# Start of the kernel and differential attention: sums moved from TensorE to VectorE, a new order of projections and heads

## The chip, the cores and the metric

The kernel runs on one core of one Trainium2 chip. The metric is the device time of one execution in microseconds (us). TensorE (PE) multiplies matrices, VectorE (DVE) and ScalarE (ACT) work element by element, GpSimd (POOL) and SyncE (SP) issue transfers here.

## The reference

Two transformer blocks over 256 tokens of width 1024 are computed, all in float32. What the change touches:

- The first block's modulation: `mod = silu(c) @ w_mod + b_mod`, six vectors of 1024. The first norm is `h = rms_norm(x, norm_mix) * (1 + scale_m) + shift_m`, and then `z = h @ w_in`.
- The second block's first layer, differential attention over 256 context tokens and 256 own tokens, 8 heads of two maps each:

```python
q, k, v = split(h @ w_qkv)            # for own and context tokens
q_l, k_l = axial_rope(q_l), axial_rope(k_l)
s = einsum('bqhnd,bkhnd->bnhqk', q, k) * scale
p = softmax(s)
a = p[:, 0] - lam * p[:, 1]
o = rms_norm_2(einsum('bhqk,bkhe->bqhe', a, v), subln_g) * (1 - lam_init)
x = x + g1 * (o @ w_o)
```

Before it stand a mixer with two attentions and a recurrence, its branch projections and a gated feed-forward layer; behind it a dense feed-forward layer, a Fourier mixer and eight experts, of which each token uses two.

## The kernel before, in words

**Weights.** All weights come through SP as slabs of 1 MB into raw buffers (`raw`, four slots, at the start three more that lie where `O` and `GT1` are later). A weight slab "G" is split in two parts, since a product is made of three passes: ACT copies it to `whi` (L1234, `act_hi`), DVE subtracts and writes `wlo` (L1812, `dve_lo`), and then PE has it. There are three such pairs, so the split of slab g+3 waits until PE is through slab g. A slab of the modulation weights "M" isn't split: DVE multiplies its rows by the entries of `csil` and adds them up in `macc` (L1836 for the first, L1839 for the others, `dve_mslabs`), and PE sums over the partitions with four short matmuls (L696, `pe_mods`), whose result DVE adds to the bias (L1857, `dve_mods`). The raw slot is free for SP when DVE has read it. The order of all slabs is the list `st_order`, the slots of the first ten are the list `early`.

**The start.** The first four modulation vectors' groups (2, 3, then 0, 1; two M slabs each) don't go this way: `pe_direct` (L710) multiplies each raw slab on PE, 16 weight loads with a moving operand of one column. Groups 2 and 3 give the scale (`dve_coeff`), 0 and 1 the shift. `pe_start` goes: transpose of `csil`'s rows, group 2, a transpose of vectors, group 3, the transposes of x (L747) with the sums of squares (L723, L726), group 0. The modulated x is written by `modulation`: `scaled` (L1878, DVE), high part `HH` (L1276, ACT), low part `HL` (`low`, L1885, DVE). `pe_mixer` multiplies the first two slabs together, chunk k by chunk k (`gemm2`, L625 to L627), and does group 1 between k = 3 and k = 4.

**Differential attention.** `pe_attention`, `act_attention` and `dve_attention` walk through 25 units. Each quarter c of the columns has five: k over context tokens, k over own tokens, q, v over context, v over own, each 48 matmuls of 256 columns (20 units, 12 slabs). After each unit the engines do `side(unit)`: rotations (`pe_rope` L963, `dve_rope` L2197 to L2205), the steps of heads, and modulation sums. A head h has steps 0 to 4, at units 5·(h // 2) + 4 + h % 2 onward: scores of query block 0 (PE L939, DVE maximum L2215), scores of block 1 and transposes of block 0 (PE L929), transposes of block 1, values (L947), norm (L952). Two heads run one unit apart, and the last ones in units 20 to 24, which have no projection. Between, DVE's side is in two parts: the maxima before `dve_lo` and `dve_mslabs`, the softmax's division and difference (L2221 to L2227) behind them, while ACT does the exponentials (L1559). At the end all heads are split to `HH2` and `HL2` (L1379, L2021), and the output projection "wo" runs over its four slabs one after the other. PE's PSUM banks are taken in rings: four for projections (`A_G`), three for the heads (`A_T`), one for the sums of squares (`A_L`); a bank is taken only after its last reader is done.

Everything is written out by hand: each engine works its list in order, and waits are semaphores.

Of the kernel before, what the change touches and what calls it, by code (L numbers as in the profile page):

```python
# [15 lines left out]
S = 256  # L16
# [183 lines left out]
def build(nc, a, out):  # L200
# [5 lines left out]
    with ctx:  # L206
# [121 lines left out]
        raw_read = Count(sem("raw_read_by_pe"))  # L328
# [41 lines left out]
        for c in range(4):  # L370
            for c0 in (4 + c, c, 8 + c):
                order += gslabs(wqkv, 8, 256 * c0, ("qkv", c0))
# [20 lines left out]
        st_order = first[:4] + order[0:2] + first[4:] + order[2:3]  # L393
# [4 lines left out]
        early = (6, 7, 8, 0, 1, 2, 3, 6, 7, 8)  # L398
        for i, entry in enumerate(st_order):
            st.add(entry, early[i] if i < 10 else (i - 10) % NR)  # L400
# [25 lines left out]
        for i, entry in enumerate(order):  # L426
            s_ = i % (NR + NX)
            st.add(entry, (s_ + first_moe - 10) % NR if s_ < NR else s_)
# [10 lines left out]
        direct = {i for i, (kind, t, *_) in enumerate(st.plan) if kind == "M" and t[0] == 0 and t[1] < 4}  # L439
# [52 lines left out]
        HEAD0 = 6  # L492
        SPANS = ((0, 128), (128, 256))


        def sp_weights(q, i0, i1):
            for i in range(i0, i1):
                _, _, src, nk, w = q.plan[i]
                s_ = q.slot[i]
                if q is st and q.prev[i] in direct:  # L500
                    sp.wait_ge(*(yield from raw_read.of(q.prev[i])))
                elif q.prev[i] is not None:
# [155 lines left out]
        def gemm2(ring, keys, tags, xh, xl, ready, between=None):  # L658
# [5 lines left out]
            for k in range(8):  # L664
                if between and k == 4:
                    between()
# [21 lines left out]
        def pe_mods(ring, slot):  # L688

            while due(pmod[0], slot):  # L690
# [8 lines left out]

        def pe_direct(ring, n):  # L700

            d, g, last, _ = mlist[n]
            u = take(ring, "mod", n)
            for i in (last - 1, last):
                pe.wait_ge(st.raw_in[st.slot[i]], 16 * st.use[i])
                v = raw[st.slot[i]][:, :].rearrange("p (k n) -> p k n", k=4)
                for j in range(4):
                    for k in range(4):
                        kk = 4 * (i + 1 - last) + k
                        t = pe.matmul(u.t[:, j:j + 1], v[:, k, j * 128:(j + 1) * 128], csil[:, kk:kk + 1], start=(j == 0 and kk == 0),  # L710
                                      stop=(kk == 7), skip_group_check=True)
                t.then_inc(raw_read.mark(i), 1)
            u.told = raw_read.now()
            pmod[0] = n + 1
# [16 lines left out]
        def pe_start():  # L731
# [4 lines left out]
            pe.wait_ge(*(yield from N.of("csil")))  # L736
            pe_direct(Z_T, 0)
# [3 lines left out]
            pe_direct(Z_T, 1)  # L741
# [11 lines left out]
            pe_direct(Z_T, 2)  # L753
# [81 lines left out]
        def pe_mixer():  # L835
            yield from gemm2(Z_G, (("z", 0), ("z", 1)), (("z", zjob[0][2]), ("z", zjob[1][2])), HH, HL,
                             lambda k: xlo_done.of("h0", k), lambda: pe_direct(Z_T, 3))
# [82 lines left out]
        A_G, A_T, A_L = (0, 1, 2, 3), (4, 5, 6), (7,)  # L920

        def pe_da(h, step):

            for qb in range(2):
                if step == qb + 1:
                    u = take(A_T, "a_p", h, qb)
                    pe.wait_ge(*(yield from dve_step.of("a_p", h, qb)))
                    for j in range(4):
                        t = pe.transpose(u.t[:, j * 128:(j + 1) * 128], PP[(2 * h + qb) % 3][:, 0, j * 128:(j + 1) * 128], ident)  # L929
                    t.then_inc(u.fill(), 1)  # L930
            for qb in range(2):
                if step == qb:
                    if step == 0:
                        pe.wait_ge(*(yield from dve_step.of("rope", "q", h // 2)))
                        pe.wait_ge(*(yield from dve_step.of("rope", "k", h // 2)))
                    for n in range(2):
                        u = take(A_T, "a_s", h, qb, n)
                        r0 = 64 * n
                        pe.matmul(u.t[:, :], Q2[r0:r0 + 64, h, qb * 128:qb * 128 + 128], K2[r0:r0 + 64, h, :],  # L939
                                  start=True, stop=True).then_inc(u.fill(), 1)  # L940
            if step == 3:
                u = take(A_T, "a_o", h)
                for n in range(2):
                    pe.wait_ge(*(yield from N.of("v2", h // 2, n)))
                    pe.wait_ge(*(yield from N.of("at", h, n)))
                for j in range(4):
                    t = pe.matmul(u.t[:, 0:S], V2[:, j, h * 128:(h + 1) * 128], AT[h % 2][:, j, :], start=(j == 0), stop=(j == 3))  # L947
                t.then_inc(u.fill(), 1)
            if step == 4:
                u = take(A_T, "a_n", h)  # L950
                pe.wait_ge(*(yield from sq_done.of("a", h)))
                pe.matmul(u.t[:, 0:S], one[:, :], sqb[h % 2][:, 0:S], start=True, stop=True).then_inc(u.fill(), 1)  # L952
                N.note(("sq_free", "a", h), u.told)
# [12 lines left out]
        def pe_attention():  # L966
            def side(unit):
                c, k = divmod(unit, 5)
                if k == 2 and c < 4:
                    yield from pe_rope("k", c)  # L970
                if k == 3 and c < 4:
                    yield from pe_rope("q", c)
                for h in range(8):
                    step = unit - (5 * (h // 2) + 4 + h % 2)
                    if 0 <= step < 5:
                        yield from pe_da(h, step)
                yield from pe_mods(A_T, st.slab_done.n - 1)

            for c in range(4):
                h, l, nk = yield from slab(st, ("qkv", 4 + c))  # L980
                us = [take(A_G, "k2", c, m) for m in range(2)]
                for n, (xh, xl, name) in enumerate(((HHc, HLc, "hc"), (HH2, HL2, "h2"))):
# [7 lines left out]
                    if n:  # L990
                        t.then_inc(st.slab_done.mark(st.pg - 1), 1)
                        us[0].told = us[1].told = st.slab_done.now()
                    yield from side(5 * c + n)
                yield from gemm(A_G, ("q2", c), ("qkv", c), 1, HH2, HL2, None, 7)
                yield from side(5 * c + 2)
                h, l, nk = yield from slab(st, ("qkv", 8 + c))
                for n, (xh, xl) in enumerate(((HHc, HLc), (HH2, HL2))):
                    u = take(A_G, "v2", c, n)
# [1675 lines left out]
```

## Time and profile before

| | |
|---|---|
| median of 3 runs | 2256.78 us (2253.92 to 2257.61) |
| the profiled execution | 2251.45 us, its span 2250.1 us |
| PE busy | 2140.3 us (95% of the span) |
| DVE busy | 1689.0 us (75%) |
| ACT busy | 1260.5 us (56%) |
| granted TensorE clock, mean | 0.963 of full |
| DMA | 580.73 MB, mean 258 GB/s |
| share of PE in the chain that ended last | 83% (DVE 9%, ACT 4%) |

Matmuls overlap in the pipeline, so a duration in the timeline is longer than the distance to the next start: of the 256-column matmuls each is shown as 0.28 us, and the next begins 0.12 us later at full clock. Distances between starts are the measure of what PE costs. A row's bracket tells how long the engine was idle before it, and what ended that.

### The profile page before, as it was taken

The page shows a single profiled execution, that of the slowest core. Times are in us where ns is not written, and L with a number is a line of the kernel's source. Part 1 is how long each engine was busy: PE and PEld are TensorE (multiplying, and loading weights), DVE is VectorE, ACT ScalarE, POOL GpSimd, SP SyncE. Part 2 cuts the span into 40 slices and gives each one's busy share as a digit, 9 for nine tenths or more (in the row PEclk, how much of TensorE's full clock was granted, in tenths as well). Part 3 has the DMA queues.
Part 4 walks back from the last instruction along what each step waited for, and adds up shares of the span by engine and source line. Part 5 has one row for each costly group of instructions (what it writes and reads, how often), then busy time and mean ns, then how long its engine had stood idle before and what let it go on. Part 6 is the DMA issues. An engine that isn't in the chain of part 4 may idle for free.

```text
span 2250.1 us, 31050 instructions
## 1 busy us (share of the span) xinstructions
PE 2140.3 (95%) x12897; PEld 1897.6 (84%) x12897; DVE 1689.0 (75%) x1809; ACT 1260.5 (56%) x1266; POOL 39.4 (2%) x77
## 2 busy tenths in 40 slices
PE   8999999989999978999998999999999999999997
PEld 8887899889997866999988788887888878888886
DVE  1477688699765664787644888888888978888886
ACT  2347753545343433434343677776777767777775
POOL 3001000000000000000000000000000000000000
PEclk9899999989999988999998999999999999999999
DMA  8574476467764332688843899999899989999994
GB/s 280 169 223 114 134 244 208 155 203 252 239 199 138 113 127 80 217 302 273 272 132 122 301 355 355 364 352 362 318 357 357 362 318 357 363 355 362 367 369 154
DMA packets 332802, 580.73 MB, mean 258 GB/s; under 512 B 10357, under 2 KB 150155, under 8 KB 332656
## 3 DMA queue, kind: packets, MB, share of 16 engines
q1 hardware_dynamic: 329152, 572.57, 73.0%
q0 software_dynamic: 3008, 5.78, 1.1%
q8 instruction: 105, 1.72, 0.3%
q10 hardware_dynamic: 496, 0.33, 0.1%
q14 instruction: 41, 0.34, 0.0%
HBM read 577.56 MB, written 1.07 MB: 257 GB/s over the span
## 4 chain that ended last, share of the span: by engine, by line
PE 83%; DVE 9%; ACT 4%; issue 3%; DMA 0%; SPq 0%; DVEq 0%; ACTq 0%
PE bk L631 14%; PE bk L633 14%; PE bk L632 14%; PE bk L625 9%; PE bk L627 9%; PE bk L626 9%; DVE macc L1839 2%; DVE wlo L1812 2%; PE bk L710 2%; ACT whi L1234 2%; PE bk L696 1%; PE bk L1126 1%; DVE uc L2154 1%; PE bk L681 1%; PE bk L683 1%
## 5 line engine op out<-in xcount | busy, mean ns | idle before, releaser
L1812 DVE TENSOR_TENSOR wlo<-raw,whi 128x2048 fp32r<-128x2048 f32 x475 | 1080.6, 2277 | 281.7 <-ACT whi L1234 281.0
L1234 ACT CAST whi<-raw 128x2048 fp32r<-128x2048 f32 x475 | 902.4, 1901 | 413.3 <-PE bk L633 271.6
L625 PE MATMUL bk<-HH,whi 128*128 128x256 f32 x1544 | 454.0, 294 | 11.3 <-DVE HL L1885 8.3
L626 PE MATMUL bk<-HL,whi 128*128 128x256 f32 x1544 | 443.8, 287 | 0.0
L627 PE MATMUL bk<-HH,wlo 128*128 128x256 f32 x1544 | 443.5, 287 | 0.0
L631 PE MATMUL bk<-whi,xh 128*128 128x512 f32 x896 | 356.9, 398 | 4.9 <-DVE wlo L1812 4.9
L633 PE MATMUL bk<-wlo,xh 128*128 128x512 f32 x896 | 351.4, 392 | 0.0
L632 PE MATMUL bk<-whi,xl 128*128 128x512 f32 x896 | 351.0, 392 | 0.0
L625 PEld LDWEIGHTS bk<-HH,whi 128*128 128x128 f32 x1544 | 304.0, 197 | 20.6 <-issue 17.9
L626 PEld LDWEIGHTS bk<-HL,whi 128*128 128x128 f32 x1544 | 304.1, 197 | 1.7 <-issue 1.0
L627 PEld LDWEIGHTS bk<-HH,wlo 128*128 128x128 f32 x1544 | 303.5, 197 | 0.0
L631 PEld LDWEIGHTS bk<-whi,xh 128*128 128x128 f32 x896 | 169.6, 189 | 40.1 <-DVE wlo L1812 6.6
L633 PEld LDWEIGHTS bk<-wlo,xh 128*128 128x128 f32 x896 | 169.4, 189 | 36.3
L632 PEld LDWEIGHTS bk<-whi,xl 128*128 128x128 f32 x896 | 169.7, 189 | 33.8
L1839 DVE SCALAR_TENSOR_TENSOR macc<-raw,csil,macc 128x512 f32<-128x512 f32 x252 | 188.9, 751 | 7.7
L631 PE MATMUL bk<-whi,tth 128*128 128x512 f32 x448 | 177.5, 396 | 1.7 <-DVE ttl L2437 1.7
L633 PE MATMUL bk<-wlo,tth 128*128 128x512 f32 x448 | 177.7, 397 | 0.0
L632 PE MATMUL bk<-whi,ttl 128*128 128x512 f32 x448 | 177.5, 396 | 0.0
L625 PE MATMUL bk<-FH,whi 128*128 128x256 f32 x400 | 114.3, 286 | 0.0
L626 PE MATMUL bk<-FL,whi 128*128 128x256 f32 x400 | 113.1, 283 | 0.0
L627 PE MATMUL bk<-FH,wlo 128*128 128x256 f32 x400 | 113.0, 283 | 0.0
L631 PEld LDWEIGHTS bk<-whi,tth 128*128 128x128 f32 x448 | 84.3, 188 | 22.1 <-DVE ttl L2437 1.9
(366 smaller groups left out, 2579.3 us busy)
## 6 DMA issues: line engine op xcount, KB each, us to landing
raw<-in_moe_w SPq DMA_DIRECT2D x336, 1024.0 KB, 5.7
raw<-in_ada_w SPq DMA_DIRECT2D x48, 1024.0 KB, 5.2
raw<-in_ff_w SPq DMA_DIRECT2D x40, 1024.0 KB, 5.4
raw<-in_w_in SPq DMA_DIRECT2D x29, 1024.0 KB, 5.4
raw<-in_w_mod SPq DMA_DIRECT2D x24, 1024.0 KB, 5.5
raw<-in_w_up SPq DMA_DIRECT2D x22, 1024.0 KB, 5.2
raw<-in_attn_w_qkv SPq DMA_DIRECT2D x12, 1024.0 KB, 5.3
raw<-in_w_branch SPq DMA_DIRECT2D x8, 1024.0 KB, 5.3
```

What stands on the lines that cost most here:

```text
L625: pe.matmul(o, sh, mh, start=start, stop=False, skip_group_check=True)
L626: pe.matmul(o, sh, ml, start=False, stop=False, skip_group_check=True)
L627: return pe.matmul(o, sl, mh, start=False, stop=stop, skip_group_check=True)
L631: pe.matmul(o, sh, mh, start=start, stop=False, skip_group_check=True)
L632: pe.matmul(o, sl, mh, start=False, stop=False, skip_group_check=True)
L633: return pe.matmul(o, sh, ml, start=False, stop=stop, skip_group_check=True)
L681: pe.matmul(o, xh[:, k, c], h[:, k, :], start=(k == 0), stop=False)
L683: t = pe.matmul(o, xh[:, k, c], l[:, k, :], start=False, stop=(k == 7))
L710: t = pe.matmul(u.t[:, j:j + 1], v[:, k, j * 128:(j + 1) * 128], csil[:, kk:kk + 1], start=(j == 0 and kk == 0), stop=(kk == 7), skip_grou ...
L1234: act.copy(whi[k][:, :n], raw[q.slot[i]][:, :n]).then_inc(q.hi_done.mark(g), 1)
L1812: dve.tensor_tensor(wlo[k][:, :n], raw[q.slot[i]][:, :n], whi[k][:, :n].bitcast(F), ALU.subtract).then_inc(q.taken.mark(i), 1)
L1839: t = dve.scalar_tensor_tensor(out=acc[:, :], in0=v[:, j, :], scalar=sc, in1=acc[:, :], op0=ALU.mult, op1=ALU.add)
```

## The change

1. Start: `pe_direct` is gone. The eight M slabs of groups 2, 3, 0, 1 go through `dve_mslabs` and `pe_mods` like the others. The stream's order and slots of the first ten slabs change. `pe_mixer`'s first two slabs are worked in halves: slab 0 for k 0 to 3, slab 1 for k 0 to 3, the sums of group 1, then both for k 4 to 7.
2. Attention: the 20 projection units get an order of their own (`units`), with q and k ahead of v, and tables tell after which unit a head's scores (`score_at`), values (`value_at`) and the rotations (`rope_at`) come. All four scores of a head come together, the transposes of its two blocks one and two units later. On DVE a head's maxima and softmax stand together, ahead of `dve_lo` and `dve_mslabs` of the unit. Projections use three banks, all the rest five.
3. Output projection: the heads are split one by one into `HHc` and `HLc`; slabs 0 and 1 are worked together, chunk by chunk, with the last units' side work (20, 21, 22) before chunks 1, 3 and 4.

```diff
-        st_order = first[:4] + order[0:2] + first[4:] + order[2:3]
+        st_order = first[:6] + order[0:2] + first[6:] + order[2:3]
-        early = (6, 7, 8, 0, 1, 2, 3, 6, 7, 8)
+        early = (6, 7, 8, 0, 1, 2, 3, 0, 6, 8)
...
+        units = [("k", 0, 0), ("k", 0, 1), ("q", 0, 1), ("k", 1, 0), ("k", 1, 1), ("q", 1, 1), ("v", 0, 0), ("v", 0, 1), ("k", 2, 0), ("k", 2, 1),
+                 ("q", 2, 1), ("v", 1, 0), ("v", 1, 1), ("k", 3, 0), ("k", 3, 1), ("q", 3, 1), ("v", 2, 0), ("v", 2, 1), ("v", 3, 0), ("v", 3, 1)]
+        score_at, value_at = (4, 5, 7, 8, 12, 13, 17, 18), (8, 9, 13, 14, 18, 19, 20, 21)
+        rope_at = {2: ("k", 0), 3: ("q", 0), 5: ("k", 1), 6: ("q", 1), 10: ("k", 2), 11: ("q", 2), 15: ("k", 3), 16: ("q", 3)}
...
-        A_G, A_T, A_L = (0, 1, 2, 3), (4, 5, 6), (7,)
+        A_G, A_T = (0, 1, 2), (3, 4, 5, 6, 7)
...
+            yield from gemm2(A_G, (("wo", 0), ("wo", 1)), (("wo", 0), ("wo", 1)), HHc, HLc, lambda k: xlo_done.of("a", k),
+                             {1: lambda: side(20), 3: lambda: side(21), 4: lambda: side(22)})
+            for c in (2, 3):
+                yield from gemm(A_G, ("wo", c), ("wo", c), 1, HHc, HLc, None, 7, c == 3)
...
+            dve.wait_ge(*(yield from N.of("csil")))
+            yield from dve_mslabs(st.gi[0] - 2)
             yield from dve_mods(-1, 2)
             yield from dve_coeff("h0", 0, "norm_mix", 0, 2)
+            yield from dve_mslabs(st.gi[0])
             scaled, low = modulation("h0", X, HH, HL, 0, 0, 0, sqb)
             for c in range(6):
                 yield from scaled(c)
-            for g in range(2):
-                yield from dve_lo(st, g)
             yield from dve_mods(-1, 3)
+            yield from dve_lo(st, 0)
             for c in range(2):
                 yield from low(c)
                 yield from scaled(6 + c)
             for c in range(2, 4):
                 yield from low(c)
+            yield from dve_lo(st, 1)
+            yield from dve_mslabs(st.gi[2])
             yield from dve_mods(-1)
...
+            for unit in range(23):
+                if unit < 20:
+                    yield from dve_mods(g - 1)
+                if unit in rope_at:
+                    yield from dve_rope(*rope_at[unit])
+                if unit in score_at:
+                    yield from dve_da_max(score_at.index(unit))
+                    yield from dve_da_softmax(score_at.index(unit))
+                for h in range(8):
+                    if unit == value_at[h] + 1:
+                        yield from dve_da_norm(h)
+                for h in {18: (0, 1, 2, 3), 20: (4,), 21: (5,), 22: (6, 7)}.get(unit, ()):
+                    yield from dve_da_split(h)
+                if unit < 20 and units[unit][2] == 1:
+                    yield from dve_lo(st, g + NP)
+                    yield from dve_mslabs(st.gi[g + NP + 1])
+                    g += 1
```

PE's list at the start, before (HH and HL are the parts of the modulated x, whi and wlo those of a weight slab):

```order
L735 MATMUL bk<-cst,crow 128x24
L710 MATMUL bk<-csil,raw_84 128x1 x16
L710 MATMUL bk<-csil,raw_85 128x1 x16
L740 MATMUL bk<-cst,vn_123 128x128
L710 MATMUL bk<-csil,raw_86 128x1 x16
L710 MATMUL bk<-csil,raw_49 128x1 x16
L747 MATMUL bk<-cst,xn 128x128 x12
```

and now:

```order
L720 MATMUL bk<-cst,crow 128x24
L723 MATMUL bk<-cst,vn_123 128x128
L697 MATMUL bk<-one,macc_70 128x1 x4
L697 MATMUL bk<-one,macc_71 128x1 x4
L730 MATMUL bk<-cst,xn 128x128 x12
```

The 64 products of groups 2 and 3 have gone from PE, and eight short sums over DVE's results stand in their place.

DVE's list of attention at head 0, before (sr holds a head's maxima and sums, pp its exponentials):

```order
L2215 TENSOR_REDUCE sr_158<-bk 128x1 x2
L2217 TENSOR_SCALAR sr_158<-sr_158 128x2
L1812 TENSOR_TENSOR wlo_58<-raw_49,whi_55 128x2048
L1836 TENSOR_SCALAR macc_71<-raw_50,csil 128x512
L1839 SCALAR_TENSOR_TENSOR macc_71<-raw_50,csil,macc_71 128x512 x3
L2221 RECIPROCAL sr_158<-sr_158 128x2
L2223 TENSOR_TENSOR sr_158<-sr_158,lt 128x1
L2225 TENSOR_SCALAR pp_153<-pp_153,sr_158 128x512
L2227 SCALAR_TENSOR_TENSOR pp_153<-pp_153,sr_158 128x512
```

and now:

```order
L2229 TENSOR_REDUCE sr_158<-bk 128x1 x2
L2231 TENSOR_SCALAR sr_158<-sr_158 128x2
L2229 TENSOR_REDUCE sr_159<-bk 128x1 x2
L2231 TENSOR_SCALAR sr_159<-sr_159 128x2
L2240 RECIPROCAL sr_158<-sr_158 128x2
L2242 TENSOR_TENSOR sr_158<-sr_158,lt 128x1
L2244 TENSOR_SCALAR pp_153<-pp_153,sr_158 128x512
L2246 SCALAR_TENSOR_TENSOR pp_153<-pp_153,sr_158 128x512
L2240 RECIPROCAL sr_159<-sr_159 128x2
L2242 TENSOR_TENSOR sr_159<-sr_159,lt 128x1
```

The slab's split and the modulation sums, which stood between a block's maxima and its softmax, now follow after both blocks of the head.

PE's list between the last projection to v and the output projection, before (at are transposed probabilities, V the values, K and Q keys and queries):

```order
L952 MATMUL bk<-sqb_78,one 128x256
L939 MATMUL bk<-K_148,Q_147 128x512 x2
L929 MATMUL bk<-cst,pp_153 128x128 x4
L939 MATMUL bk<-K_148,Q_147 128x512 x4
L929 MATMUL bk<-cst,pp_154 128x128 x4
L929 MATMUL bk<-cst,pp_155 128x128 x4
L939 MATMUL bk<-K_148,Q_147 128x512 x2
L947 MATMUL bk<-at_156,V_149 128x256 x4
L929 MATMUL bk<-cst,pp_153 128x128 x4
L952 MATMUL bk<-sqb_77,one 128x256
L947 MATMUL bk<-at_157,V_149 128x256 x4
L952 MATMUL bk<-sqb_78,one 128x256
```

and now:

```order
L935 MATMUL bk<-cst,pp_154 128x128 x4
L935 MATMUL bk<-cst,pp_155 128x128 x4
L950 MATMUL bk<-sqb_77,one 128x256
L944 MATMUL bk<-at_157,V_149 128x256 x4
```

No scores are left there; of the rest, one set of transposes, three norms and two heads' values have moved to between the first chunks of the output projection.

## Rows read from the trace of the kernel before

**Rows 1.** Busy time by stretch: us, PE, PEld, DVE, ACT, POOL; clock; DMA.

```profile
0.00:7.80 7.80, 0.30 (x1) 0.19 (x2) 0.60 (x5) 2.26 (x3) 6.27 (x16) 1.00 0.73 229
...
42.40:54.00 11.60, 10.34 (x65) 10.22 (x64) 7.51 (x10) 5.51 (x7) 0.00 (x0) 0.66 0.39 123
```

**Rows 2.** Timeline of PE, start: start us, us, instruction, idle before.

```profile
7.82 13.78 PE L710 MATMUL bk<-csil,raw 128*128 128x1 f32 x64 [3.77 <-DMA raw<-in_w_mod]
...
35.22 2.80 PE L747 MATMUL bk<-cst,xn 128*128 128x128 f32 x12
...
73.60 0.58 PE L625 MATMUL bk<-HH,whi 128*128 128x256 f32 x1 [1.31 <-DVE HL L1885]
```

**Rows 3.** Slab transfers by window: issue durations and starts, then issue to landing.

```profile
L506 SPq DMA_DIRECT2D raw<-in_w_mod x1: 1080/1080/1080, 3.4 to 3.4; - x1
DMA to landing us min/median/max: 14.5/14.5/14.5
...
L506 SPq DMA_DIRECT2D raw<-in_w_in x2: 727/3894/7062, 8.2 to 8.9; - x2
DMA to landing us min/median/max: 17.2/18.1/19.1
```

**Rows 4.** Timeline of DVE, 35 to 57 and 84 to 94 us.

```profile
43.75 2.47 DVE L1878 SCALAR_TENSOR_TENSOR sqb<-X,nA,rst 128x256 f32<-128x256 f32 x6 [7.92 <-ACT rst L1264]
...
84.98 0.48 DVE L1836 TENSOR_SCALAR macc<-raw,csil 128x512 f32<-128x512 f32 x1
...
90.60 3.10 DVE L1839 SCALAR_TENSOR_TENSOR macc<-raw,csil,macc 128x512 f32<-128x512 f32 x4
```

**Rows 5.** Page, section 5: the split's first part (busy, mean ns, idle before).

```profile
L1234 ACT CAST whi<-raw 128x2048 fp32r<-128x2048 f32 x475 | 902.4, 1901 | 413.3 <-PE bk L633 271.6
```

**Rows 6.** Busy time by stretch, attention: columns as in Rows 1.

```profile
646.80:836.30 189.50, 174.93 (x1170) 153.01 (x1168) 118.57 (x209) 70.14 (x126) 2.05 (x4) 0.94 0.42 136
836.30:871.10 34.80, 16.31 (x51) 8.92 (x49) 19.21 (x38) 14.14 (x34) 0.00 (x0) 0.75 0.18 60
871.10:905.70 34.60, 31.79 (x241) 31.04 (x241) 14.29 (x23) 10.61 (x14) 1.97 (x3) 0.91 0.38 116
```

**Rows 7.** Timeline of PE, attention: first row of 144 matmuls and what follows.

```profile
646.81 0.47 PE L625 MATMUL bk<-HHc,whi 128*128 128x256 f32 x1
...
664.40 0.38 PE L963 MATMUL bk<-K,cs 128*128 128x256 f32 x1
...
763.26 1.03 PE L963 MATMUL bk<-K,cs 128*128 128x256 f32 x4
764.13 1.89 PE L947 MATMUL bk<-at,V 128*128 128x256 f32 x8
765.86 0.60 PE L929 MATMUL bk<-cst,pp 128*128 128x128 f32 x4
...
781.35 1.13 PE L939 MATMUL bk<-K,Q 64*128 64x512 f32 x4
```

**Rows 8.** PE's groups by line, 646.8 to 871 us: busy, mean ns, idle before.

```profile
L939 PE MATMUL bk<-K,Q 64*128 64x512 f32 x64 | 30.2, 768 | 9.8 <-ACT pp L1559 5.2 <-ACT at L1549 4.6
...
L929 PE MATMUL bk<-cst,pp 128*128 128x128 f32 x64 | 10.7, 303 | 18.7 <-DVE pp L2227 18.7
```

**Rows 9.** Timeline of DVE, 836 to 864 us: a split, one head's last block.

```profile
837.76 2.28 DVE L1812 TENSOR_TENSOR wlo<-raw,whi 128x2048 fp32r<-128x2048 f32 x1
...
859.26 1.29 DVE L2215 TENSOR_REDUCE sr<-bk 128x1 f32<-128x512 f32 x2 [3.27 <-PE bk L939]
...
862.33 0.17 DVE L2221 RECIPROCAL sr<-sr 128x2 f32<-128x2 f32 x1 [1.58 <-ACT pp L1559]
...
863.25 0.75 DVE L2227 SCALAR_TENSOR_TENSOR pp<-pp,sr 128x512 f32<-128x512 f32 x1
```

**Rows 10.** Waits of SP's own queue, whole span: us in total, times, longest.

```profile
SPq L506 <- DVE wlo L1812: 1747.3, 467, 39.4
```

**Rows 11.** Busy time by stretch, experts: columns as in Rows 1.

```profile
1277.00:2220.00 943.00, 930.70 (x4257) 768.45 (x4256) 821.24 (x556) 678.57 (x488) 0.00 (x0) 0.99 0.97 350
```

More of the change, by code:

```diff
@@ L499, in sp_weights @@
                 s_ = q.slot[i]
[L500 to L502 removed]
+                if q.prev[i] is not None:
                     sp.wait_ge(*(yield from q.taken.of(q.prev[i])))
@@ L664, in gemm2 @@
             for k in range(8):
-                if between and k == 4:
-                    between()
+                if between and k in between:
+                    yield from between[k]()
                 pe.wait_ge(*(yield from ready(k)))
@@ L686, in build, with pe_mods @@
         pmod = [0]
-        def pe_mods(ring, slot):
-            while due(pmod[0], slot):
+        def pe_mods(ring, slot, most=99):
+            while due(pmod[0], slot) and pmod[0] < most:
                 d, g, i, _ = mlist[pmod[0]]
@@ L698, in pe_mods @@
                 pmod[0] += 1
[L700 to L714, printed above, removed]
         def pe_stats(ring, name, c, halves=False):
@@ L918, in pe_ffn, with pe_da_scores @@
             yield from pe_stats(F_L, "x2", 6, True)
-        A_G, A_T, A_L = (0, 1, 2, 3), (4, 5, 6), (7,)
-        def pe_da(h, step):
+        A_G, A_T = (0, 1, 2), (3, 4, 5, 6, 7)
+        def pe_da_scores(h):
+            pe.wait_ge(*(yield from dve_step.of("rope", "q", h // 2)))
+            pe.wait_ge(*(yield from dve_step.of("rope", "k", h // 2)))
             for qb in range(2):
[L925 to L942, printed above, removed]
-                for n in range(2):
[L944 to L953, printed above, removed]
@@ new lines, in pe_da_values, with pe_da_norm @@
+        def pe_da_values(h):
+            u = take(A_T, "a_o", h)
+            for n in range(2):
+                pe.wait_ge(*(yield from N.of("v2", h // 2, n)))
+                pe.wait_ge(*(yield from N.of("at", h, n)))
+            for j in range(4):
+                t = pe.matmul(u.t[:, 0:S], V2[:, j, h * 128:(h + 1) * 128], AT[h % 2][:, j, :], start=(j == 0), stop=(j == 3))
+            t.then_inc(u.fill(), 1)
+        def pe_da_norm(h):
+            u = take(A_T, "a_n", h)
+            pe.wait_ge(*(yield from sq_done.of("a", h)))
+            pe.matmul(u.t[:, 0:S], one[:, :], sqb[h % 2][:, 0:S], start=True, stop=True).then_inc(u.fill(), 1)
+            N.note(("sq_free", "a", h), u.told)
@@ L989, in pe_attention @@
                                       k == 0 and n == 0, k == 7)
[L990 to L998, printed above, removed]
[L999 to L1004 removed]
+                elif kind == "q":
+                    us = [take(A_G, "q2", c)]
+                    for m in range(2):
+                        for k in range(8):
+                            cols = slice(m * 128, (m + 1) * 128)
+                            t = three(us[0].t[:, m * S:(m + 1) * S], (h[:, k, cols], l[:, k, cols]), (xh[:, k, :], xl[:, k, :]),
+                                      k == 0 and m == 0, k == 7)
+                else:
+                    us = [take(A_G, "v2", c, n)]
+                    natural(us[0].t[:, 0:256], h, l, xh, xl, 0)
+                    t = natural(us[0].t[:, 256:512], h, l, xh, xl, 1)
```

318 lines of the change are left out of this document (166 added, 152 removed).

## The prediction
> **What bounds the kernel now.** I read the busy times by stretch first, then PE's timeline at both changed places, then who waits for whom. PE is busy nearly throughout, so what counts is which of its work is dear and where it stands still. In the first 35 us PE does little but 1-column products: 64 matmuls in 13.78 us, and x is not transposed before 35.22 [rows 2]. DVE has nothing to do there: its first large work starts at 43.75 after 7.92 us idle [rows 4]. Attention takes 646.8 to 905.7, 258.9 us [rows 6]. In its first 189.5 us PE is mostly busy; from 836.3 to 871.1 it is busy for 16.3 of 34.8 us, with heads alone and no projection beside them. The heads' matmuls wait for each other's results, 18.7 us for softmax parts and 9.8 for the exponentials and copies [rows 8].
>
> **The sum is made against the profiled execution**, 2251.45 us, which is 5.3 us (0.24%) below the median of 2256.78; I take the same difference off the median. What a measurement can tell from no change is about 0.2%, 4.5 us.
>
> **Start, first half.** Four groups leave PE: 4 times 64 products. DVE gets eight slabs of four instructions, 0.48 for the first of a group and about 0.77 for the others, so 2.8 and 3.1 us for a group's two slabs [rows 4]. The first slab is there at 7.8 [rows 2], the fourth at 3.4 + 14.5 = 17.9 [rows 3]: one per 3.4 us, slower than DVE takes them. So the fourth is summed at 17.9 + 3.1 = 21.0. PE's short sum (four weight loads and matmuls) I take as 1 us, and x is transposed from 22.0 instead of 35.22: **13.2 us earlier**. From there to DVE's scaling was 43.75 - 35.22 = 8.5 us; it is now 30.5.
>
> **Start, second half.** Slots 1 and 2 now take group 0 at the place where the first two weight slabs were, landing at 8.2 + 17.2 = 25.4 and 8.9 + 19.1 = 28.0 [rows 3]; summed by 31.3, no later than the statistics. Weight slabs 0 and 1 follow in the queue at about 31 and 34. Slab 1 waits for its raw slot, which DVE leaves at 21: hidden. ACT's copies take 1.9 each [rows 5]: done at 32.9 and 35.9; both stand ahead of HH in ACT's list. DVE: six scalings 2.5 to 33.9, split of slab 0 (2.3) to 36.2, then four low parts and two scalings, 6 times about 0.5, to 39.8; PE starts at 36.9. Split of slab 1 to 42.1, group 1 (landed by 40) 6 us to 48.1. PE has slab 0's half in 24 times 0.12 us (below) at full clock and twice that at half, I take 5, and waits for slab 1's split; its half is over by 47.2. Then sum (1 us), HH, HL: chunk 4 can start at 50.4. Before it was 73.60 [rows 2]: **23.2 us earlier**. What follows is the same, but slab 0 now ends 24 matmuls before slab 1 instead of together with it, so ACT casts the next slab (1.9) beside PE and not ahead of the vectors' copies for which PE waits. Term: 23.2 + 1.9 = **25 us** (18 to 28). The work that hides DVE's sums is the arrival of slabs; without that cover it would be 23.6 us of DVE.
>
> **Attention, PE alone.** 144 matmuls run from 646.81 to 664.40 [rows 7], so a unit is 5.86 us, 0.12 each. Twenty units: 117.2. A head: scores 1.1, two transposes 0.5 each, values 1.7, norm 0.45 (half a rotation), 4.25 in all, 34 for eight; eight rotations of 0.87, 7; two modulation sums 2 [rows 7]. Out projection 23.4 with three sums of squares 1.4. From the end of its last matmul to the end of the stage stays as it is: 34.6 - 26 = about 8.3 [rows 6], because the stage's last stretch holds the same four slabs. Sum: **193 us** with no wait, 66 below the 258.9 of now. This is the upper bound.
>
> **Attention, waits that come.** A head on DVE is: maxima 1.29 and on to the reciprocal at 862.33, 3.1 us after 859.26, with 1.58 idle for ACT's exponentials; end of block 0 at 864.0, 4.8 after its start; block 1 another 1.7: **6.5 us in one piece** [rows 9]. Before, the split and the sums filled that idle time; that cover is gone, and 8 heads pay 1.6 more on DVE, with the split (2.3) and the sums (3) of the unit behind. In units 5 to 9 DVE has four heads 26, three splits 7, three sums 9, two rotations 4.4 (five instructions of 0.4 to 0.7): 46 us. PE has five units 29.3 and side work of 13: 42. So PE stands about 4.5 us, first where a short modulation sum needs the bank that rotation k1 left for a DVE still busy with slab 80. At heads 3, 5 and 7, second of their pairs, the transposes of block 0 come 1 us late each; in the output projection chunk 0 waits 0.6 for the split of heads 0 to 3, and chunk 6 1.5 for head 7's norm and split. Together 9 us. Weight slabs are never late: each split comes two to three units before its use. SP waits for DVE's splits [rows 10], now a few us later in a unit, and its slab has two units more. The granted clock was 0.94, 0.75 and 0.91 in the three stretches [rows 6]; most of those dips stood behind pauses that go, and I leave 2 us for new ones. Term: 66 - 9 - 2 = **55 us** (42 to 62).
>
> **Behind the changed places** nothing else differs, and each stage starts with the same slabs in hand. In the experts the DMA share is 0.97 [rows 11]: they are bound by transfers. But their slabs can't be fetched ahead: SP stood 1747 us in 467 waits for a split by DVE [rows 10], so the stream shifts with the stages before.
>
> **Sum:** 25 + 55 = 80. Own execution 2251.45 - 80 = 2171.5, **median 2177 us**.
>
> **Rivals.**
>
> *The start stays at half clock.* PE will be nearly idle until 22 us. For it: after the 1-column products the granted clock was 0.66 from 42.4 to 54.0; against: it was 1.00 in the first 7.8 us with PE idle [rows 1]. If all of x's transposes and sums (7.2 us before 42.4) and the last 48 matmuls (5.9 at full clock) run at 1.2 instead of 2.4 GHz, up to 10 us are lost: gain 70, 2187 us. The Trainium skill, "TensorE: Matmul & The Clock Gate", Part 1, says that the default state is throttled and that activity releases it. By that rule this rival would hold; the first row of rows 1 speaks against it, since nothing had released the clock there. Chance 0.17.
>
> *DVE sets the pace of attention.* If the piece of 6.5 us makes PE wait 3 us more at each of eight heads (the waits of now were 2 to 3 where a softmax was late), 24 us of the gain go: 2201 us. For it: DVE's 138 us of work in the stage against 160 of PE, in clusters; against: each head has one to two units of 5.86 before its transposes. Chance 0.13.
>
> *The gain is absorbed.* If the experts' slabs came on a schedule of their own, the time would stay at 2257. Against it stand rows 10. Chance 0.02.
>
> *Slower than before.* Rings and orders knot: PE at each head waits until DVE is through a whole unit (6.5 + 2.3 + 3 and a rotation, 14 us), because the next bank of the ring of five was last read by DVE. 8 times 14 is 112, against 66 and 25 gained: 21 us slower, 2278. It decides from 11 us per head on. Only one such take is in the order, in unit 5, and it costs 4.5. Chance 0.02.
>
> That the change doesn't do what it says can be excluded: the lists show the products gone from PE and the tail moved.
>
> **Numbers.** Forecast as summed 0.66, 2177 us. Range: the low end has both upper bounds, 28 + 62 = 90, 2167, and the profiled execution may be nearer to the median, 5 us less: 2161. The high end is the DVE rival, 2202. Faster by over 0.2%: 0.66 + 0.17 + 0.13 = 0.96. Same 0.02, slower 0.02.
>
> **What would show it.** Right: x transposed at 20 to 24 us, chunk 4 of the first slabs at 48 to 53; first matmul of attention's k about 25 us earlier than 646.8; the stage 200 to 210 us long, no gap of 8 us between projections and output projection, waits of PE for pp under 8 us. Wrong: chunk 4 after 58, or a stage over 220 us, or an experts' stretch that is longer than before by what the start gained.

## The result and the profile after

| | before | after |
|---|---|---|
| median | 2257.2 us (2253.92 to 2258.16, 4 runs) | **2168.3 us** (2166.41 to 2169.77, 4 runs) |
| profiled execution | 2251.45 us | 2169.39 us, span 2167.8 |
| PE busy | 2140.3 us (95%) | 2074.4 us (96%) |
| DVE busy | 1689.0 us (75%) | 1710.9 us (79%) |
| granted TensorE clock, mean | 0.963 | 0.974 |

The ratio is 0.9608 (95% interval 0.9592 to 0.9625): 88.9 us faster by the medians, 82.1 between the two profiled executions. Forecast were 80 and 2177 us.

Busy time by stretch of the changed kernel, in the columns of [rows 1]: the start, PE's first group of 48 and what follows, attention, and the larger part of the experts.

```profile
0.00:7.80 7.80, 0.30 (x1) 0.18 (x1) 0.60 (x5) 2.52 (x3) 6.27 (x16) 1.00 0.72 232
7.80:22.30 14.50, 3.98 (x17) 3.63 (x18) 11.67 (x17) 0.51 (x2) 11.42 (x23) 1.00 1.06 354
...
36.90:61.60 24.70, 19.77 (x112) 17.95 (x113) 17.99 (x24) 9.33 (x14) 0.00 (x0) 0.77 0.69 226
...
621.00:824.00 203.00, 198.19 (x1460) 182.80 (x1460) 151.17 (x273) 94.27 (x177) 4.56 (x8) 0.98 0.49 157
...
1145.00:1796.00 651.00, 638.54 (x2935) 528.55 (x2936) 555.16 (x401) 464.58 (x349) 0.00 (x0) 0.99 0.94 341
```

DVE's sums now run where PE's products were, and in attention PE is busy for 198.2 of 203 us, where it was 223.0 of 258.9 [rows 6].

The timeline of PE at the start, to be held against [rows 2]:

```profile
14.40 1.87 PE L697 MATMUL bk<-one,macc 128*128 128x1 f32 x8 [3.29 <-DVE macc L1852]
20.67 1.84 PE L697 MATMUL bk<-one,macc 128*128 128x1 f32 x8 [4.39 <-DVE macc L1852]
22.37 2.80 PE L730 MATMUL bk<-cst,xn 128*128 128x128 f32 x12
24.96 1.06 PE L708 MATMUL bk<-sqb,one 128*128 128x256 f32 x2
...
28.59 0.59 PE L708 MATMUL bk<-sqb,one 128*128 128x256 f32 x2
...
36.88 0.55 PE L626 MATMUL bk<-HH,whi 128*128 128x256 f32 x1 [5.61 <-DVE HL L1898]
...
47.29 1.02 PE L697 MATMUL bk<-one,macc 128*128 128x1 f32 x8 [2.36 <-DVE macc L1852]
49.63 0.58 PE L626 MATMUL bk<-HH,whi 128*128 128x256 f32 x1 [1.31 <-DVE HL L1898]
```

x is transposed at 22.37 (before 35.22), and the last row, chunk 4 of the first two slabs, stands at 49.63 (before 73.60). The first matmul of the output gate comes at 301.2 in place of 326.4, of attention's k at 621.5 in place of 646.8: **the start gave 25.2 us**, and all of it arrives.

DVE's timeline in the same stretch shows what replaced PE's products:

```profile
11.24 3.11 DVE L1852 SCALAR_TENSOR_TENSOR macc<-raw,csil,macc 128x512 f32<-128x512 f32 x4 [0.46 <-DMA raw<-in_w_mod]
...
14.98 5.54 DVE L1852 SCALAR_TENSOR_TENSOR macc<-raw,csil,macc 128x512 f32<-128x512 f32 x7
...
31.61 2.46 DVE L1891 SCALAR_TENSOR_TENSOR sqb<-X,nA,rst 128x256 f32<-128x256 f32 x6 [1.54 <-ACT rst L1275]
```

The scaling of x begins at 31.61, where it stood at 43.75 [rows 4].

In attention the waits of [rows 8] are gone. PE's waits from 621 to 824 us (total, times, longest) are one line:

```profile
PE bk L697 <- DVE sqb L2214: 2.0, 1, 2.0
```

The stage lasts from 621.53 to 824.01, **202.5 us instead of 258.9: 56.4 gained**. What it is made of I worked out by adding up, along PE's timeline, the distance from each row's start to the next, less the idle time in the next row's bracket; the 2.8 us for HL at the stage's end count as waits:

| attention stage, us | split products | other matmuls | waits of PE | stage |
|---|---|---|---|---|
| before | 149.8 | 73.2 | 35.8 | 258.9 |
| after | 143.2 | 54.4 | 4.8 | 202.5 |

Of the 56.4 us, 31.0 are waits; 25.4 are the same matmuls done in less time, 18.8 of them the heads' and the other small ones, many of which stood in the stretch with a clock of 0.75 before [rows 6].

The feed-forward layer behind it took 254.9 us instead of 252.1 (824.01 to the Fourier mixer's first matmul at 1078.9; before 905.68 to 1157.8) with the same waits and less clock at its ends. The experts, from the first product with their permutation (L1100, at 1145.2; before at 1224.6) to the end of the span, took 1022.6 instead of 1025.5. Two executions of one kernel differ by nearly as much: the changed kernel, executed again, took 252.6 and 1025.0.

### The profile page after: what moved, and what is told of

It reads as the page before. It is cut to its first block, busy times and chain, and to the rows that moved or that the text cites. A ratio compares the mean times of both kernels' runs of the same rounds, so it can differ in the third digit from the quotient of the medians.

```text
span 2167.8 us, 30644 instructions
## 1 busy us (share of the span) xinstructions
PE 2074.4 (96%) x12673; PEld 1846.4 (85%) x12673; DVE 1710.9 (79%) x1845; ACT 1260.4 (58%) x1270; POOL 39.5 (2%) x77
## 4 chain that ended last, share of the span: by engine, by line
PE 83%; DVE 10%; ACT 4%; issue 3%; DMA 0%; SPq 0%; DVEq 0%; ACTq 0%
PE bk L632 14%; PE bk L634 14%; PE bk L633 14%; PE bk L626 9%; PE bk L628 9%; PE bk L627 9%; DVE macc L1852 3%; DVE wlo L1825 2%; ACT whi L1245 2%; PE bk L697 1%; PE bk L1137 1%; PE bk L682 1%; DVE uc L2171 1%; PE bk L683 1%; PE bk L684 1%
## 5 line engine op out<-in xcount | busy, mean ns | idle before, releaser
L626 PE MATMUL bk<-HH,whi 128*128 128x256 f32 x1480 | 432.8, 292 | 13.2 <-DVE HL L1898 12.6
L627 PE MATMUL bk<-HL,whi 128*128 128x256 f32 x1480 | 423.5, 286 | 0.0
L628 PE MATMUL bk<-HH,wlo 128*128 128x256 f32 x1480 | 423.3, 286 | 0.0
L626 PEld LDWEIGHTS bk<-HH,whi 128*128 128x128 f32 x1480 | 289.4, 196 | 19.1 <-issue 16.4
L627 PEld LDWEIGHTS bk<-HL,whi 128*128 128x128 f32 x1480 | 289.3, 195 | 1.4 <-issue 0.7
L628 PEld LDWEIGHTS bk<-HH,wlo 128*128 128x128 f32 x1480 | 288.8, 195 | 0.0
L1852 DVE SCALAR_TENSOR_TENSOR macc<-raw,csil,macc 128x512 f32<-128x512 f32 x280 | 209.9, 751 | 9.3 <-DMA raw<-in_w_mod 0.5
```

Source lines behind the costliest of these rows:

```text
L626: pe.matmul(o, sh, mh, start=start, stop=False, skip_group_check=True)
L627: pe.matmul(o, sh, ml, start=False, stop=False, skip_group_check=True)
L628: return pe.matmul(o, sl, mh, start=False, stop=stop, skip_group_check=True)
L1852: t = dve.scalar_tensor_tensor(out=acc[:, :], in0=v[:, j, :], scalar=sc, in1=acc[:, :], op0=ALU.mult, op1=ALU.add)
```

## The experiments

Experiments 1 to 4, 5 to 8 and 9 to 12 each share their runs of the kernel before, whose medians were 2256.93, 2256.57 and 2256.85 us. The changed kernel was timed again beside the last of them: 2169.82 us, ratio 0.9619 (0.9606 to 0.9632). Differences in us are to the kernel before in experiments 1 and 2, to the changed kernel's 2168.3 us in 3 to 8, and to its second median of 2169.82 in 12.

**1. The start alone.** The kernel before with the new stream order, the sums by `dve_mslabs` and the halves; attention as it was.

```diff
-            pe_direct(Z_T, 1)
+            yield from pe_mods(Z_T, -1, 2)
...
-            pe_direct(Z_T, 2)
+            yield from pe_mods(Z_T, -1, 3)
...
```

> The kernel before with the new start alone. By the sum of the prediction the start is worth 25 us: 2257 - 25 = 2232 us, with the first 72-matmul group of the mixer at about 61.7 us and attention beginning 25 us earlier and 259 us long as before. Rival (the two parts share a gain, so that either alone brings most of it): below 2215 us. Rival (the start's gain is given back by later stages unless attention changes too): above 2245 us.

Measured: 2228.06 us (2226.36 to 2232.65), ratio 0.9872 (0.9856 to 0.9889): **-28.9 us**. The output gate's first matmul is at 300.8, attention's at 622.3, so the trace has 24.5 us of it ahead of attention. The 4 us beyond are not found in a stage: attention, unchanged, took 262.1 us here, not less than before.

**2. Attention alone.** The kernel before with the new `pe_attention`, `act_attention`, `dve_attention` and the order of weight slabs that they need.

```diff
-            for unit in range(20, 25):
-                yield from side(unit)
...
+                if unit in score_at:
+                    yield from pe_da_scores(score_at.index(unit))
...
```

> The kernel before with the new attention alone. By the sum it is worth 55 us, in the profile of the change 56.4: 2257 - 56 = 2201 us, attention beginning at 646.8 and 202 to 205 us long. If the parts didn't add up, the two single gains would sum to clearly more or less than the 89 us that both together brought; the sum of terms says 80 to 82, and the rest would be differences between executions and of the granted clock.

Measured: 2194.99 us (2186.53 to 2196.6), ratio 0.9718 (0.9699 to 0.9736): **-61.9 us**. Its stage lasts 205.5 us (647.25 to 852.73), with the same two waits of PE as in the full change, 2.0 and 2.8. The two gains add up to 90.8 us, and together they brought 88.9: within the intervals, which are some 4 us to either side for each ratio, the two parts of the change are independent, and nothing behind them absorbs either.

**3. Side work ahead of the output projection.** Units 20 to 22's side work stands before it and no longer between its chunks.

```diff
-                             {1: lambda: side(20), 3: lambda: side(21), 4: lambda: side(22)})
+            for unit in (20, 21, 22):
+                yield from side(unit)
...
```

> The change with the side work of the last three units ahead of the output projection instead of between its chunks. The theory that the heads' earlier scores made the gain, and that the interleaving covers only the three norms' waits for ACT's squares: 3 waits of about 1.2 us and no other, 3 to 5 us slower than the change. Rival, that the interleaving is what removed the bare stretch of 34.8 us: 15 to 25 us slower.

Measured: 2171.0 us (2166.45 to 2173.89), ratio 0.9619 (0.9605 to 0.9634), +2.7 us. Beside the waits of 2.0 and 2.8 us that the change has too, the stage has three, 2.5 us together, each for ACT's squares:

```profile
783.74 0.67 PE L950 MATMUL bk<-sqb,one 128*128 128x256 f32 x2 [0.67 <-ACT sqb L1582]
787.38 0.67 PE L950 MATMUL bk<-sqb,one 128*128 128x256 f32 x2 [1.25 <-ACT sqb L1582]
790.35 0.67 PE L950 MATMUL bk<-sqb,one 128*128 128x256 f32 x2 [0.57 <-ACT sqb L1582]
```

So the interleaving with the output projection hides about 2.5 us and no more; the stage is 205.3 us long. The rival (15 to 25) falls. The time itself is within 0.2% of the change. What carries the stage is then, by elimination, that the scores of all eight heads have their turn among the projections. This is argued and not shown: no run changes the order of units, the places of the scores or the division of the banks alone.

**4. The old cover inside a head.** DVE's split and sums of a unit stand between the maxima and the softmax again, where the kernel before filled DVE's idle time for ACT with them; ACT casts ahead of the exponentials.

```diff
                 if unit in score_at:
                     yield from dve_da_max(score_at.index(unit))
+                if unit < 20 and units[unit][2] == 1:
+                    yield from dve_lo(st, g + NP)
+                    yield from dve_mslabs(st.gi[g + NP + 1])
+                    g += 1
+                if unit in score_at:
                     yield from dve_da_softmax(score_at.index(unit))
...
```

> The change with DVE's split and modulation sums back between a head's maxima and its softmax (and ACT's cast ahead of the exponentials), at the five heads whose unit has both. The theory that PE needs the softmax early: DVE saves 1.6 us of idle time per such head, but the first block's softmax comes 5.3 us later less that idle time, and PE waits at the transposes, 2 to 3 us at each of five heads: 8 to 15 us slower. Rival, that the lost cover is what limits DVE: 4 to 8 us faster.

Measured: 2186.97 us (2184.51 to 2189.58), ratio 0.9691 (0.9677 to 0.9704), **+18.7 us**. Three of PE's five waits for a softmax, and the sum of the five in the view of waits:

```profile
662.87 1.09 PE L935 MATMUL bk<-cst,pp 128*128 128x128 f32 x4 [2.79 <-DVE sr L2240]
677.65 0.63 PE L935 MATMUL bk<-cst,pp 128*128 128x128 f32 x4 [2.70 <-DVE sr L2240]
695.97 0.63 PE L935 MATMUL bk<-cst,pp 128*128 128x128 f32 x4 [2.78 <-DVE sr L2240]
```

```profile
PE bk L935 <- DVE sr L2240: 14.1, 5, 3.0
```

The direction was right, the size was not: the stage is 218.2 us, 15.8 longer. Waits grew by 12.1, and the matmuls other than the split products by 4.2. The remaining 3 us of the 18.7 are not in the stage. The edit moves two things, DVE's work and ACT's cast; DVE's rows at head 0, first of the changed kernel and then of this run, tell them apart:

```profile
656.68 0.17 DVE L2240 RECIPROCAL sr<-sr 128x2 f32<-128x2 f32 x1 [0.19 <-ACT pp L1561]
```

```profile
661.06 0.16 DVE L2240 RECIPROCAL sr<-sr 128x2 f32<-128x2 f32 x1
```

ACT is through with the head's exponentials at 658.0 in the one and 657.8 in the other, so it is the 5.4 us of work on DVE that hold the result back for which PE waits. And the expectation's 1.6 us of idle time per head are not there to be filled: since the maxima of both blocks stand together, DVE waits 0.19 to 0.20 us for ACT at each of the eight heads of the changed kernel.

**5. Two modulation sums one slab later**, to take away the one wait that was left.

```diff
-                 ((1, 8), (75, 76), 78), ((1, 9), (77, 78), 80), ((1, 10), (79, 80), "x3"), ((1, 11), (81, 82), "x3"),
+                 ((1, 8), (75, 76), 79), ((1, 9), (77, 78), 81), ((1, 10), (79, 80), "x3"), ((1, 11), (81, 82), "x3"),
```

> Edit: two modulation sums of attention, due after slabs 78 and 80, each due one slab later (79, 81); nothing else. My theory: the only wait of PE in the attention stage of the changed kernel (2.00 us for DVE's squares, at 665.62, before a sum of 8 products) is there because the sum takes a bank that DVE reads last, and PE falls to half clock behind it (48 matmuls in 7.24 us in place of 6.0). So the wait falls under 0.5 us, the stage is 2 to 3 us shorter than 202.5, and the time is 2 to 3 us under the changed kernel's. Rival: the squares are late for whatever comes next in the ring of banks, so the wait only moves to the next rotation or head: the stage stays within 1 us of 202.5 and the time within 1 us.

Measured: 2170.99 us (2168.5 to 2173.86), ratio 0.9628 (0.9615 to 0.9641). The theory falls. The rival's mechanism holds, a little outside its bound of 1 us for the stage: the wait has moved to the next consumers and grown to 3.5, of which these two rows are 3.0 and a wait of 0.5 before the scores at 693.23 is the rest:

```profile
671.83 0.63 PE L935 MATMUL bk<-cst,pp 128*128 128x128 f32 x4 [1.82 <-DVE sr L2240]
680.66 1.99 PE L928 MATMUL bk<-K,Q 64*128 64x512 f32 x8 [1.16 <-DVE Q L2222]
```

DVE was behind there; the sum was only what met it first. The stage is 203.7 us, 1.2 longer.

**6. The first two slabs chunk by chunk**, not in halves.

```diff
+            yield from gemm2(Z_G, (("z", 0), ("z", 1)), (("z", zjob[0][2]), ("z", zjob[1][2])), HH, HL,
+                             lambda k: xlo_done.of("h0", k), {4: lambda: pe_mods(Z_T, -1)})
...
```

> Edit: the first two slabs chunk by chunk together, as before the change, with the sum of the second group ahead of chunk 4; all else of the start as changed. My theory: PE's first matmul comes only when both slabs are split, near 42 instead of 36.9 us, and the 48 matmuls (6 us at full clock, 8 at half) then end at 48 to 50, when the second group's sum is there anyway (47.3): chunk 4 at 50 to 52 instead of 49.6. The next slab's cast then stands ahead of the vectors' copies again. So the halves are worth 1 to 4 us; time 1 to 4 us above the changed kernel's. Rival, that the halves carry the start: the 5 us by which the first matmul comes later is lost in full, with the 1.9 of the cast, 7 us.

Measured: 2173.82 us (2168.86 to 2174.86), ratio 0.9632 (0.9616 to 0.9648): 5.5 us above the change's first median, 4.0 above its second. From PE's timeline:

```profile
41.58 0.55 PE L626 MATMUL bk<-HH,whi 128*128 128x256 f32 x1 [9.93 <-DVE wlo L1809]
...
51.34 0.39 PE L626 MATMUL bk<-HH,whi 128*128 128x256 f32 x1 [1.31 <-DVE HL L1882]
```

Chunk 4 comes 1.7 us later, as expected, and the output gate 3.5 us later (304.64 against 301.17): the halves are worth 1.7 us at chunk 4 and about as much again behind it. In seven executions with the new start and no edit to it, chunk 4 stands at 49.4 to 49.9 and the output gate at 298.5 to 301.4, so the first number is firm and the second is good to some 2 us.

**7 and 8. Matmuls in PE's idle gaps.** Twelve matmuls that nobody reads (4, 5 and 3) in the gaps of the start, then the same together with edit 5.

```diff
+        def busy(n):
+            for _ in range(n):
+                pe.matmul(banks[4][:, 0:384], ident, cst[:, 0:384], start=True, stop=True)
...
```

> Edit: 12 matmuls of 384 columns whose result nobody reads, put into PE's idle gaps of the start: 4 after the first sum of products, 5 after the third, 3 ahead of the fourth. My theory: the half clock of 25.0 to 27.5 us and of the first 20 of the 48 matmuls follows from PE's standing idle before; kept at work, the transposes and sums of x take their 0.59 us for two matmuls throughout, and the 48 matmuls that took 8.05 and 8.48 us take 6 to 7. What lies on the path from x's transposes to chunk 4 is at most the 1 us of sums and the 2.5 us of the second 48: the time is 0 to 3.5 us under the changed kernel's. Rival, clock follows something else than PE's idle time: the durations stay and the time is 0 to 1 us above.

> Both edits together: the matmuls in the idle gaps of the start, and the two modulation sums one slab later. If both theories hold, the two gains add: 2 to 6 us under the changed kernel's time (2162 to 2166 us). If either rival holds its part falls away; if both do, the time is the changed kernel's within 1 us.

Measured: warm 2165.11 us (2160.52 to 2168.32), ratio 0.9596 (0.9581 to 0.9612); warm_sum 2168.95 us (2168.25 to 2169.13), ratio 0.9616 (0.9603 to 0.9629). From the timeline of warm:

```profile
22.35 1.51 PE L736 MATMUL bk<-cst,xn 128*128 128x128 f32 x12
24.32 0.70 PE L708 MATMUL bk<-sqb,one 128*128 128x256 f32 x2 [0.46 <-ACT sqb L1266]
...
49.16 0.58 PE L626 MATMUL bk<-HH,whi 128*128 128x256 f32 x1 [1.32 <-DVE HL L1906]
```

The 12 transposes take 1.51 us instead of 2.80, the sums of squares 0.70 and 0.59 instead of 1.06, the first group of 48 matmuls 6.3 us beside 0.9 of waiting, instead of 7.9. The transposes took 2.80 us in all seven executions without filling matmuls, and the first group 7.3 to 7.9, so both are the edit's doing. The second group of 48 isn't: it still begins with matmuls shown as 0.41 us and takes 7.25 us from its start to the next row's, where the change has 8.3, but change_again, unedited, has 7.3. Chunk 4 moves by 0.5 us only: little of what became faster was on the path.

**9 to 12.** The kernel before profiled again, the change and warm timed side by side, and DVE's maxima computed twice.

> The kernel before, unedited, executed and profiled once more. My theory: the profiled execution of 2251.45 us was a quick one, 5.6 us under the median of some 20 others; so this one comes out at 2254 to 2260, its mean granted clock is 0.960 to 0.962 and not 0.963, and the extra time is spread over the long stages between the changed places (clock, not waits): first matmul of attention's k at 647 to 651 in place of 646.8. Rival: 2251 to 2253 again, and the profiling itself makes the difference to the timed runs.

> The changed kernel, unedited, timed on the chip of this call, so that its edits can be held against it within one call. Expected 2166 to 2171 us, 86 to 91 under the kernel before; ratio within 0.9592 to 0.9625.

> The 12 unread matmuls in PE's idle gaps of the start once more, now beside the changed kernel. If their 3 us under it is real, it comes again: 1 to 4 us under change_again, with the chunk 4 of the first slabs at 49.2 in place of 49.6 and the 48 matmuls behind it in 7.2 in place of 8.5 us. If it was the spread of executions, the two lie within 1 us.

*before_again* took 2259.92 us with a granted clock of 0.959, 8.5 us over the first profiled execution. My theory had the sign and the size, but not the place: attention begins at 647.4 (646.8), so nothing is lost before it; its stage takes 264.1 us instead of 258.9, which is 5.3 of the 8.4 between the spans. Its waits are as long as before (35.9 against 35.8 us), but the other matmuls take 78.3 us instead of 73.2. The same two groups of PE's timeline, first in the execution of the prediction, then in the new one:

```profile
705.18 1.12 PE L939 MATMUL bk<-K,Q 64*128 64x512 f32 x2 [1.52 <-ACT at L1549]
706.24 1.05 PE L696 MATMUL bk<-one,macc 128*128 128x1 f32 x8
```

```profile
705.81 2.07 PE L939 MATMUL bk<-K,Q 64*128 64x512 f32 x2 [1.52 <-ACT at L1549]
707.81 1.86 PE L696 MATMUL bk<-one,macc 128*128 128x1 f32 x8
```

Behind the same wait of 1.52 us the same matmuls take twice as long in one execution. From there to PE's next wait of over 1 us, for rst, the first needs 28.4 us at a granted clock of 1.00, the second 31.5 at 0.89: 3.1 of the 5.3 us. The same attention took 262.1 us in start_only. The changed attention isn't free of this either: with the same waits of 4.8 us it took 202.5, 202.4, 202.3, 201.8, 205.4 and 205.5 us in six executions (after, change_again, warm, interleaved, warm_again, attention_only).

*change_again* and *warm_again*: 2169.82 us (2167.44 to 2172.06) and 2167.36 us (2164.29 to 2168.02), ratios 0.9619 (0.9606 to 0.9632) and 0.9605 (0.9592 to 0.9618). The 10 runs of warm and warm_again average 2166.0 and the 9 of the change 2169.0 us. The output gate's first matmul is at 299.5 and 297.7 with the filling matmuls, 301.2 and 300.3 without, but at 298.5 in tail_bare, which has none. So 2 to 3 us may be real, yet 0.14% is under what the intervals can tell apart, and warm_sum doesn't show them. I don't call it a better version.

*max_twice*:

```diff
+                    dve.tensor_reduce(s[:, 9 + n:10 + n], B.at["a_s", h, qb, n].t[:, :], AX, ALU.max)
...
```

> Edit: each of the 32 row maxima of attention (0.64 us on DVE, four for a head) is computed twice, the first result unread: 2.56 us more of DVE for each head, 20.5 us in all. My theory: PE sets the pace, and DVE's results come 0.5 to 0.7 us ahead of it at heads 3, 5 and 7 and some 1.9 to 2.2 ahead at the others. So PE waits about 2 us at each of three heads and 0.4 to 0.7 at each of the other five: 8 to 9 us, with half clock behind the waits 9 to 13 us on the time. Rival, DVE is the engine behind in the whole stage: 20 us or more. Rival, there is slack enough that the order of work and not DVE's amount counts: under 4 us.

Measured: 2189.08 us (2185.6 to 2192.88), ratio 0.97 (0.9684 to 0.9715), **+19.3 us**. The number is nearer to the first rival's; the waits tell which part of each holds:

```profile
PE bk L935 <- DVE pp L2247: 9.8, 7, 3.1
PE bk L697 <- DVE sqb L2214: 3.7, 1, 3.7
```

Of the seven waits for pp, four last 0.2 us and three about 3 (2.88, 3.15, 2.89, at heads 3, 5 and 7). So the first head of a pair has some 2.4 us in hand, and the second next to none, nearly as I had it; but the second waits longer than its own 2.56 us, probably for what its predecessor could not make up. The wait before the modulation sum grew from 2.0 to 3.7. Waits grew by 11.9 us, while the stage grew by 20.6 (223.0, against 202.4 in change_again). Nearly all of the rest is matmuls that took longer (7.4 us the heads' and other small ones, 1.4 the split products), and this is clock, as busy time by stretch around head 3 shows:

```profile
700.00:707.30 7.30, 4.47 (x38) 4.23 (x36) 7.12 (x16) 3.09 (x9) 0.00 (x0) 1.00 0.70 247
707.30:712.40 5.10, 5.05 (x22) 4.43 (x22) 1.46 (x4) 1.75 (x5) 0.00 (x0) 0.67 0.02 5
712.40:720.00 7.60, 7.60 (x61) 7.47 (x60) 4.73 (x5) 4.70 (x10) 0.00 (x0) 1.00 0.09 20
```

```profile
703.87 0.60 PE L935 MATMUL bk<-cst,pp 128*128 128x128 f32 x4
707.35 1.08 PE L935 MATMUL bk<-cst,pp 128*128 128x128 f32 x4 [2.88 <-DVE pp L2247]
```

PE stands for 2.88 us at a granted clock of 1.00 (2.4 GHz), and what it does next has 0.67, which is mostly the lower level of 1.2 GHz: the same four transposes, 0.60 before the wait and 1.08 behind it. My 9 to 13 us had the waits 3 us and the clock some 5 us too low.

## Why the prediction was right, point by point

**Start, first half** (13.2 us): 12.9. The fourth slab was summed at 20.5 (21.0 forecast), x transposed at 22.37 (22.0).

**Start, second half** (23.2 us): 24.0. Scaling from 31.6 (30.5), PE's first matmul at 36.88 (36.9), split of slab 1 done at 41.2 (42.1), group 1 summed at 47.1 (48.1), chunk 4 at 49.63 (50.4). The 1.9 us for the halves came as 1.2 (25.2 at the output gate), a difference of two executions that is good to some 2 us. The chain was right because each link was a duration from the trace set behind the later of two arrivals.

**Attention, PE alone** (193 us): too low. PE's own work with the wait at the end is 200.5 us. The step "20 units by 5.86, a head 4.25" took durations from a stretch at full clock. The split products needed 143.2 us where I had 140.6, the rest 54.4 and the 2.8 of the end, where I had 52.7. Of these 7.5 us, 2 were in the sum as clock.

**Attention, waits** (9 us): 2.0. The one at the bank that rotation k1 left came, at 665.62, and took 2.00 us instead of 4.5; the 1 us at heads 3, 5 and 7 and the 2 in the output projection did not. In the changed kernel the first block of head 3 leaves DVE at 699.01 and is transposed at 699.73, as two rows show, of DVE and of PE:

```profile
698.26 0.75 DVE L2246 SCALAR_TENSOR_TENSOR pp<-pp,sr 128x512 f32<-128x512 f32 x1
```

```profile
699.73 1.04 PE L935 MATMUL bk<-cst,pp 128*128 128x128 f32 x8
```

The margin is 0.7 us (0.5 at head 5, 0.7 at head 7), where I had -1. The 1.6 us more on DVE that I had each head pay are not in the trace either (0.2 us, see experiment 4), though the piece as a whole, 6.5 us, measured 6.3. Of the gain, the waits that didn't come give 7 us more, PE's own work takes back 5.5: that the term of 55 comes so near to the 56.4 of the trace is luck, two wrong sizes that nearly cancel.

**The step that missed most** is the one in front of the sum: "I take the same difference off the median". The profiled execution of before lay 5.8 us under the median of its four runs, that of the change lies 1.1 above its own. This accounts for 6.8 of the 8.9 us between forecast gain and measured gain. before_again shows where much of such a difference sits: the attention stage of before took 258.9, 262.1 and 264.1 us in three executions, by the clock behind its pauses. My 55 was read from the quickest of them. By the execution that one takes on either side, attention gave 53 to 62 us; alone it gave 61.9 by its medians. Whether the changed stage is steadier, for want of pauses, is not shown: its six executions lie 3.7 us apart, the three of before 5.3.

**Rivals.** *The start stays at half clock*: no, but it was not empty. The first row of [rows 1] was my evidence against it, a clock of 1.00 with PE idle. The changed kernel has 1.00 up to 22.3 us as well, and even in the stretch from 22.3 to 25.0; yet there the 12 transposes take 2.80 us, and 1.51 with matmuls ahead of them (warm). A granted clock in an idle stretch says nothing of the matmuls that end it. The Trainium skill, "TensorE: Matmul & The Clock Gate", Part 1, says that the throttled state is the default and that activity releases it; the durations agree with that. It cost little. The 48 matmuls of the second group lost 2.4 us (8.3 against 5.9; 1.3 to 2.4 over seven executions). The sums of x's squares were on the path in this execution, since DVE's scaling stood 1.54 us for ACT's rst behind them (the last of DVE's rows above); in change_again they ran at 0.6 us from 25.8 on and DVE didn't wait, and yet chunk 4 came at 49.83. Up to 10 us in all were in the rival. *DVE sets the pace*: not with this order, but only by a margin of 0.5 to 0.7 us at three heads, as the rows above show; covered and max_twice show what it costs when the margin goes. *Absorbed*: refuted; 25.2 us of the start are still there at 621.5, and the experts take as long as before. That transfers bound them, as I wrote from a DMA share of 0.97, no run shows: PE too was busy for 930.7 of those 943 us [rows 11]. *Slower, rings knot*: one bank wait of 2.0 us is all there is of it.

## What to carry to other kernels

In a stage where one engine waits for short chains of others, order the work so that each chain is whole and early, and let the engine that is waited for leave its bulk work until behind the chain: bulk work of 5.4 us within the chain made PE wait 14.1 us in all here. Look first whether there is idle time to fill: two blocks' steps put together had already filled it, down to 0.2 us. A pause of PE costs more than its length, since the matmuls behind it may run at a lower clock (11.9 us of waits took 20.6), so price the removal or the making of a pause by both. Before adding up against one profiled execution, profile the kernel a second time: the same stage with the same waits varied by 5.3 of 259 us before the change, and by 3.7 of 202 after it.

## What the runs showed of the hardware

- Here the granted clock of a stretch was no guide to the speed of the first matmuls in it: 1.00 from 22.3 to 25.0 us, with twelve transposes in 2.80 us and not 1.51.
- Behind a wait of 2.0 us the 48 matmuls at 666.82 took 7.1 us up to the next row's start, in place of 5.9. Behind a wait of 1.52 us two score matmuls took 1.12 us in one execution of the kernel before and 2.07 in another. In the output projection of tail_bare waits of 0.6 to 1.25 us left the pairs of squares behind them at 0.67 us.
- Moving a wait does not remove it: with the sum one slab later, 2.0 us at one place became 1.8, 1.2 and 0.5 at three others.
